# A gathered mixture of experts: the diagonal of gates and activations built on VectorE instead of ScalarE

## The chip, the cores and the metric

The kernel runs on one core of a Trainium2 chip. The metric is the device time of one execution in microseconds. All data are fp32 except indices.

## The reference

The kernel computes two transformer blocks on 256 latent and 256 context tokens of width 1024. The change touches only their last kind of layer, a product-key mixture of experts ("peer"), which runs twice:

```python
def block_fn(xb):                       # 128 tokens of width 1024
    qry = (xb @ w_query).reshape(P, 8, 2, 128)
    s = jnp.einsum('phcd,hckd->phck', qry, sub_keys)
    top_s, top_i = lax.top_k(s, 16)
    cand_s = top_s[..., 0, :, None] + top_s[..., 1, None, :]      # 16 x 16 pairs
    cand_i = top_i[..., 0, :, None] * 128 + top_i[..., 1, None, :]
    best_s, pos = lax.top_k(cand_s, 16)
    idx = jnp.take_along_axis(cand_i, pos, axis=-1)
    gate = jax.nn.softmax(best_s, axis=-1)
    act = jax.nn.gelu(jnp.einsum('pd,phkd->phk', xb, u_tab[idx]))
    coef = gate * act
    return jnp.einsum('phk,phkd->pd', coef, v_tab[idx])
```

Each token picks 8 x 16 = 128 experts. For each it needs a dot product with a row of `u_tab` and adds a multiple of a row of `v_tab`.

## The kernel before

A tile is 128 tokens, one per partition. Layer 0 has four tiles (0 to 3), layer 1 two (here 4 and 5). A row (`ee`, 0 to 127) is one expert for each token of the tile; `q = 128 * n + ee` counts rows in a layer. Each engine runs its own hand-written program; they meet only at semaphores. `wait_ge` waits, `then_inc(*S.up(key))` announces, and `v()` and `a()` add a wait for the engine's own last operation.

For each row:
- GpSimd (POOL, L2893) issues an indirect DMA that fetches 128 rows of 2048 numbers, u and v side by side, 1 MB, into one of seven buffers. It waits for the dot and for the matmuls of the row seven before.
- VectorE (DVE, L2909) multiplies the u half with the tokens and sums it into one column of `acts`: the dot.
- ScalarE (ACT, `act_row`, recorded at L211 as all its operations) makes three operations: GELU of that column into `coef`, `coef` times the column of `gates`, and the identity times `coef`: a 128x128 diagonal in one of four buffers `dg`.
- TensorE (PE, L2863) multiplies the diagonal with the v half in two matmuls of 512 columns (four records), accumulating over all 128 rows in two PSUM banks.

At the end of a tile VectorE waits for the last matmul and adds the result to the tokens (L2920, L2922), and only then starts the next tile's dots.

Beside the rows of a tile the next tile's experts are selected. From row 8 on (row 14 in tile 1) TensorE computes the scores (L2731, L2741) and ScalarE copies them and the next tokens out of PSUM before it turns to the row's own work (`act_select`). VectorE does one piece of `dve_select` per row, behind the dot: 48 rows of MAX8, FIND_INDEX8 and MATCH_REPLACE8 over 128 elements, two rows that add pairs (L2800), 24 rows over 256 elements (L2805 to L2811), 24 rows that look up indices (L2822, L2825, L221), and a few small ones; at row 107 ScalarE takes an Exp for the gates (`act_gates`). Tiles 3 and 5 are the last of their layers and select nothing.

Some rows carry work of neighbouring stages (`beside`): tile 0 and the first rows of tile 1 the latent half of the projection before the layer, its norm and its queries (`pe_late`, `dve_late`, `act_late`, with 16 MB of weights), tile 3 the keys of the attention that follows, tile 5 a part of the final norm.

## Time and profile before

| | |
|---|---|
| time, three runs | 4545.08 us median, 4542.48 to 4550.28 |
| the profiled execution | 4545.08 us, span 4543.3, mean granted TensorE clock 0.939 |
| busy | PE 84%, PEld 47%, DVE 62%, ACT 28%, POOL 26% of the span |
| tiles of experts | 2286 to 2674, 3007, 3331, 3664 us (layer 0); 3877 to 4212, 4534 (layer 1) |
| gathers | 768, 820 MB on the queue they share with GpSimd's other loads |

How to read it: the profile is one execution. An engine is busy while an instruction runs; PE is the matmuls, PEld the weight loads, DVE VectorE, ACT ScalarE, POOL GpSimd. The share of the 16 DMA engines' time is the DMA share. The granted clock is in parts of full speed. In the rows below "idle before" is the time for which the engine stood before the operation, and the arrow names what ended it. All operands lie in one allocation named `arena` (SBUF) or in `bank` (PSUM).

### The profile page before, as it was taken

What the parts mean: (1) busy time and instruction counts of PE and PEld (TensorE: products, weight loads), DVE (VectorE), ACT (ScalarE), POOL (GpSimd) and SP (SyncE); (2) the same over time, 40 slices, a digit from 0 to 9 for tenths busy, and PEclk for the clock granted to TensorE, in tenths of its full rate; (3) what the DMA queues carried; (4) which work ended last, traced back from release to release, by engine and by line L of the source; (5) the groups of instructions that cost most, each with busy time, mean ns of one, the idle gap of its engine ahead of it and who ended that gap; (6) DMA issues with size and microseconds to landing.
All of it is one profiled execution on the core that took longest, in us unless ns stands there. A gap on an engine that the chain in (4) does not pass through costs nothing.

```text
span 4543.3 us, 43290 instructions
## 1 busy us (share of the span) xinstructions
PE 3794.2 (84%) x13554; PEld 2121.6 (47%) x13554; DVE 2832.7 (62%) x5670; ACT 1268.6 (28%) x3341; POOL 1197.0 (26%) x1220
## 2 busy tenths in 40 slices
PE   7879879998878898887879888777779778777777
PEld 3334437643467777676844552232223247322222
DVE  3756447767666677664667747767755546676544
ACT  1231110025311222212133333343333321333333
POOL 0001100001033343331034333333344400333333
PEclk9889999999988999889989999999999989999999
DMA  5423235544200000003289999999999942899998
GB/s 211 176 99 125 100 130 188 219 157 169 88 6 24 5 24 6 26 6 152 83 338 420 384 363 421 421 403 421 422 407 413 422 168 75 345 421 421 407 422 364
DMA packets 140150, 1073.82 MB, mean 236 GB/s; under 512 B 15504, under 2 KB 15888, under 8 KB 21520
## 3 DMA queue, kind: packets, MB, share of 16 engines
q0 software_dynamic: 112608, 820.04, 43.9%
q1 hardware_dynamic: 27312, 251.02, 14.5%
q8 instruction: 107, 1.75, 0.2%
q14 instruction: 123, 1.01, 0.1%
HBM read 1060.51 MB, written 10.49 MB: 236 GB/s over the span
## 4 chain that ended last, share of the span: by engine, by line
PE 39%; DMA 20%; DVE 19%; issue 12%; POOL 7%; ACT 2%; DVEq 0%; POOLq 0%; SPq 0%; ACTq 0%
PE bank L199 19%; DMA arena<-in_uv,arena 18%; POOL arena L2893 6%; PE bank L2863 3%; PE bank L2423 3%; DVE arena L2909 2%; PE bank L2146 2%; DVE arena L443 2%; ACT arena L211 2%; PE bank L2138 2%; PE bank L1620 2%; DVE arena L561 2%; DVE arena L217 2%; DVE arena L221 2%; PE bank L2125 1%
## 5 line engine op out<-in xcount | busy, mean ns | idle before, releaser
L2863 PE MATMUL bank<-arena 128*128 128x512 f32 x3072 | 1492.0, 618 | 390.6 <-ACT arena L211 390.1
L211 ACT ACTIVATE arena<-arena 128x1 f32<-128x1 f32 (+5 forms) x2625 | 866.2, 330 | 2055.2 <-DVE arena L2909 1155.2
L2909 DVE CUSTOM_DVE_ANT_0 arena<-arena 128x1024 f32<-128x1024 f32 x768 | 941.3, 1226 | 703.4 <-DMA arena<-in_uv,arena 690.2
L199 PE MATMUL bank<-arena 128*128 128x128 f32 (+5 forms) x4896 | 1303.7, 426 | 75.2 <-ACT arena L211 35.1
L2863 PEld LDWEIGHTS bank<-arena 128*128 128x128 f32 x3072 | 541.6, 191 | 1314.4 <-ACT arena L211 880.7
L2893 POOL DMA_INDIRECT arena<-in_uv,arena x768 | 772.5, 1006 | 1338.7 <-PE bank L2863 870.1
L199 PEld LDWEIGHTS bank<-arena 128*128 128x128 f32 (+3 forms) x4896 | 816.2, 196 | 551.7 <-issue 424.8
L211 ACT ACTIVATE arena<-bank 128x512 f32<-128x512 f32 (+3 forms) x464 | 248.2, 535 | 1081.3 <-PE bank L2125 503.3
L2208 POOL TENSOR_TENSOR arena<-arena 128x512 f32<-128x512 f32 x128 | 163.5, 1277 | 456.1 <-PE bank L2138 449.2
L443 DVE CUSTOM_DVE_ANT_0 arena<-arena 128x1024 f32<-128x1024 f32 x192 | 240.6, 1253 | 33.8 <-DMA arena<-in_w_rows 22.0
L2146 PE MATMUL bank<-arena 128*128 128x128 f32 x1024 | 159.5, 306 | 88.6 <-DVE arena L2167 88.6
L2146 PEld LDWEIGHTS bank<-arena 128*128 128x128 f32 x1024 | 142.5, 214 | 106.9 <-DVE arena L2167 98.5
L626 POOL TENSOR_SCALAR arena<-arena 128x1 f32<-128x1 f32 (+3 forms) x48 | 15.5, 323 | 648.2 <-ACT arena L211 454.0
L561 DVE SCALAR_TENSOR_TENSOR arena<-bank,arena 128x508 f32<-128x508 f32 (+2 forms) x248 | 159.0, 641 | 8.8
L2167 DVE TENSOR_TENSOR arena<-arena,bank 128x512 f32<-128x512 f32 x128 | 88.0, 687 | 113.2 <-PE bank L2138 106.3
L2138 PE MATMUL bank<-arena 128*128 128x128 f32 x1024 | 141.4, 285 | 2.2 <-issue 2.0
L217 DVE TENSOR_SCALAR arena<-bank,arena 128x256 f32<-128x256 f32 (+3 forms) x162 | 84.0, 518 | 93.3 <-PE bank L520 50.4
L2138 PEld LDWEIGHTS bank<-arena 128*128 128x128 f32 x1024 | 129.1, 196 | 17.2 <-issue 13.0
L211 ACT ACT_TABLE_LOAD x86 | 110.3, 1283 | 80.0 <-DMA arena<-gates_rest 25.3
L2423 PE MATMUL bank<-arena 128*128 128x512 f32 x256 | 131.4, 639 | 0.0
L217 DVE TENSOR_SCALAR arena<-bank 128x512 f32<-128x512 f32 x128 | 88.5, 691 | 42.8 <-PE bank L2146 32.3
L216 DVE TENSOR_SCALAR arena<-bank,arena 128x256 f32<-128x256 f32 (+5 forms) x98 | 55.3, 565 | 77.6 <-PE bank L199 60.8
(250 smaller groups left out, 2800.3 us busy)
## 6 DMA issues: line engine op xcount, KB each, us to landing
arena<-in_w_rows SPq DMA_DIRECT2D x50, 1024.0 KB, 4.9
arena<-in_w_in SPq DMA_DIRECT2D x16, 2048.0 KB, 8.2
arena<-in_wq SPq DMA_DIRECT2D x14, 2048.0 KB, 8.6
arena<-in_dn_w SPq DMA_DIRECT2D x12, 2048.0 KB, 9.0
arena<-in_w_up SPq DMA_DIRECT2D x11, 2048.0 KB, 8.0
arena<-in_dn_wo SPq DMA_DIRECT2D x8, 2048.0 KB, 11.0
arena<-in_w_rows POOLq DMA_DIRECT2D x14, 1024.0 KB, 6.3
arena<-in_uv,arena POOLq DMA_INDIRECT x768, 12.8
```

The costliest lines, as they stand in the source:

```text
L199: t = p.e.matmul(out, l, r, start=(i == 0), stop=(i == n - 1))
L211: return a().activation(out, in_, f, **kw)
L217: return v().tensor_scalar(out, a, s1, s2, op0, op1)
L443: v().tensor_tensor_reduce(trash, w[:, j, :], self.crow[r], 1.0, 0.0, ALU.mult, ALU.add, self.M[m][:, j0 + j, c:c + 1]).then_inc(*(V.up("m ...
L561: t = v().scalar_tensor_tensor(dst[:, :, o], src[:, :, f], wc(d + h), dst[:, :, o], ALU.mult, ALU.add)
L2138: t = p.e.matmul(b[:, H4[h]], N[:, H4[h]], X[:, H4[h]], start=True, stop=True)
L2146: t = p.e.matmul(b[:, H4[h]], m["Y"][d][:, H4[h]], m["XT"][d][k % 2][:, H4[h]], start=True, stop=True)
L2208: g().tensor_tensor(heads(m["N"][d], 4), heads(m["AT"][d][k % 2], 4), bc(m["masks"][:, d, l - 3, :], 1, 4), ALU.mult).then_inc(*G.up("in.N ...
L2423: t = p.e.matmul(b, self.hT[:, q, 128 * i:128 * i + 128], m["zch"][:, q, :], start=(q == 0), stop=(q == 7))
L2863: t = p.e.matmul(by[half], m["dg"][ee % 4], m["uv"][r][:, 1024 + 512 * half:1536 + 512 * half], start=(ee == 0), stop=(ee == 127))
L2893: g.e.indirect_dma_start(out=m["uv"][q % 7], out_offset=None, in_=self.I["uv"], in_offset=bass.IndirectOffsetOnAxis(ap=m["idx"][n % 2][:, ...
L2909: v().tensor_tensor_reduce(self.spare, uv[:, 0:1024], m["ht"][n % 2], 1.0, 0.0, ALU.mult, ALU.add, m["acts"][:, ee:ee + 1]).then_inc(*V.up ...
```

## The change

ScalarE keeps the GELU alone. VectorE builds the diagonal, behind the dot and the selection piece of the same row: one tensor_scalar that multiplies the identity by the column of `coef` and by the column of `gates`. It waits for ScalarE's GELU and for the matmuls of the row four before. TensorE waits for VectorE's `dg` instead of ScalarE's. ScalarE no longer waits for the gates or for a `dg` buffer; from the third tile of a layer it waits for the last diagonal of the tile two before, which read the same `coef` buffer.

```diff
--- before.py
+++ after.py
@@ -2858,7 +2858,7 @@
                 if n + 1 < nt and ee == self.select_row(m["layer"], n):
                     self.pe_select(p, m, k, n + 1, None)
                 r = (128 * n + ee) % 7
-                p.wait_ge(*A.of(k + ".dg", n, ee))
+                p.wait_ge(*V.of(k + ".dg", n, ee))
                 for half in range(2):
                     t = p.e.matmul(by[half], m["dg"][ee % 4], m["uv"][r][:, 1024 + 512 * half:1536 + 512 * half],
                                    start=(ee == 0), stop=(ee == 127))
@@ -2910,6 +2910,11 @@
                                          m["acts"][:, ee:ee + 1]).then_inc(*V.up(k + ".dot", n, ee))
                 if ee >= self.select_row(m["layer"], n):
                     next(ahead, None)
+                v.wait_ge(*A.of(k + ".act", n, ee))
+                if q > 3:
+                    v.wait_ge(*P.of(k + ".y", *divmod(q - 4, 128)))
+                v().tensor_scalar(m["dg"][ee % 4], self.ident, m["coef"][n % 2][:, ee:ee + 1],
+                                  m["gates"][n % 2][:, ee:ee + 1], ALU.mult, ALU.mult).then_inc(*V.up(k + ".dg", n, ee))
                 self.beside(n, ee, side)
             run(ahead)
             i = t0 + n
@@ -2929,25 +2934,16 @@
         self.act_gates(a, m, k, 0)
         self.act_experts(a, m, k, side)
 
-    def act_row(self, a, m, k, n, ee):
-
-        P, V, A = self.P, self.V, self.A
-        q, coef = 128 * n + ee, m["coef"][n % 2][:, ee:ee + 1]
-        a.wait_ge(*V.of(k + ".dot", n, ee))
-        act(a, coef, m["acts"][:, ee:ee + 1], ACT.Gelu).then_inc(*A.up(k + ".act", n, ee))
-        a.wait_ge(*V.of(k + ".gate", n))
-        act(a, coef, coef, ACT.Copy, scale=m["gates"][n % 2][:, ee:ee + 1]).then_inc(*A.up(k + ".coef"))
-        if q > 3:
-            a.wait_ge(*P.of(k + ".y", *divmod(q - 4, 128)))
-        act(a, m["dg"][ee % 4], self.ident, ACT.Copy, scale=coef).then_inc(*A.up(k + ".dg", n, ee))
-
     def act_experts(self, a, m, k, side):
         P, V, A, nt = self.P, self.V, self.A, m["nt"]
         for n in range(nt):
             for ee in range(128):
                 if n + 1 < nt and ee == self.select_row(m["layer"], n):
                     self.act_select(a, m, k, n + 1)
-                self.act_row(a, m, k, n, ee)
+                a.wait_ge(*V.of(k + ".dot", n, ee))
+                if n > 1:
+                    a.wait_ge(*V.of(k + ".dg", n - 2, 127))
+                act(a, m["coef"][n % 2][:, ee:ee + 1], m["acts"][:, ee:ee + 1], ACT.Gelu).then_inc(*A.up(k + ".act", n, ee))
                 if n + 1 < nt and ee == self.select_row(m["layer"], n) + self.SELECT:
                     self.act_gates(a, m, k, n + 1)
                 self.beside(n, ee, side)
```

## Rows read from the trace of the kernel before

**Rows 1.** The page: busy us of each engine, share of the span, instructions.
```profile
PE 3794.2 (84%) x13554; PEld 2121.6 (47%) x13554; DVE 2832.7 (62%) x5670; ACT 1268.6 (28%) x3341; POOL 1197.0 (26%) x1220
```

**Rows 2.** Windows, tiles 0, 5: PE, PEld, DVE, ACT, POOL; clock, DMA share, GB/s.
```profile
2286.00:2674.00 388.00, 344.98 (x1063) 198.37 (x1064) 240.82 (x520) 132.41 (x415) 154.52 (x138) 0.96 0.97 396
4212.00:4534.00 322.00, 253.60 (x512) 88.07 (x512) 162.40 (x263) 116.17 (x386) 116.52 (x124) 0.99 0.98 407
```

**Rows 3.** Timeline of a steady row, tile 2: start, duration, engine, idle before.
```profile
3201.39 1.23 DVE L2909 CUSTOM_DVE_ANT_0 arena<-arena 128x1024 f32<-128x1024 f32 x1 [0.74 <-DMA arena<-in_uv,arena]
3202.66 1.02 ACT L211 ACTIVATE arena<-arena 128x1 f32<-128x1 f32 x3 [1.48 <-DVE arena L2909]
...
3203.74 1.98 PE L2863 MATMUL bank<-arena 128*128 128x512 f32 x4 [0.52 <-ACT arena L211]
3203.88 1.22 DVE L2909 CUSTOM_DVE_ANT_0 arena<-arena 128x1024 f32<-128x1024 f32 x1 [0.26 <-DMA arena<-in_uv,arena]
```

**Rows 4.** The gather's line L2893, issue to landing, all 768.
```profile
DMA to landing us min/median/max: 5.5/12.8/14.2
```

**Rows 5.** Groups of VectorE's dots in tile 0, windows 2478:2513 and 2455:2517.
```profile
L2909 DVE CUSTOM_DVE_ANT_0 arena<-arena 128x1024 f32<-128x1024 f32 x13 | 15.9, 1225 | 2.0 <-DMA arena<-in_uv,arena 0.3
...
L2909 DVE CUSTOM_DVE_ANT_0 arena<-arena 128x1024 f32<-128x1024 f32 x21 | 25.7, 1226 | 8.4 <-DMA arena<-in_uv,arena 6.2
```

**Rows 6.** Groups by form, VectorE, windows 350:370 and 2286:4535 (mean ns).
```profile
L216 DVE TENSOR_SCALAR arena<-arena 128x128 f32<-128x128 f32 x4 | 1.1, 287 | 0.9 <-POOL arena L1193 0.9
...
L2822 DVE TENSOR_TENSOR arena<-arena 128x512 f32<-128x512 f32 x40 | 27.7, 692 | 1.5
L217 DVE TENSOR_SCALAR arena<-bank,arena 128x128 f32<-128x128 f32 x32 | 13.1, 409 | 13.3 <-PE bank L520 10.6
```

**Rows 7.** Timelines of single operations, in four places.
```profile
1246.54 1.27 POOL L2027 TENSOR_TENSOR arena<-arena 128x512 f32<-128x512 f32 x1 [144.37 <-ACT arena L211]
1247.24 0.85 DVE L216 TENSOR_SCALAR arena<-arena 128x512 f32<-128x512 f32 x1
...
1490.51 0.69 DVE L217 TENSOR_SCALAR arena<-bank 128x512 f32<-128x512 f32 x1 [1.92 <-PE bank L2146]
1491.33 0.69 DVE L1995 TENSOR_TENSOR arena<-arena,bank 128x512 f32<-128x512 f32 x1
...
2599.96 0.94 POOL L2893 DMA_INDIRECT arena<-in_uv,arena  x1 [0.32 <-PE bank L2863]
2600.44 0.23 DVE L216 TENSOR_SCALAR arena<-arena 128x128 f32<-128x128 f32 x1
...
3103.74 0.20 ACT L211 ACTIVATE arena<-arena 128x1 f32<-128x1 f32 x1 [1.46 <-DVE arena L2909]
```

**Rows 8.** Timeline of the boundary of tiles 4 and 5.
```profile
4214.78 1.23 DVE L2909 CUSTOM_DVE_ANT_0 arena<-arena 128x1024 f32<-128x1024 f32 x1 [0.17 <-DVE arena L2922]
...
4216.16 1.23 DVE L2909 CUSTOM_DVE_ANT_0 arena<-arena 128x1024 f32<-128x1024 f32 x1
...
4221.18 1.15 POOL L2893 DMA_INDIRECT arena<-in_uv,arena  x1 [8.27 <-PE bank L2863]
```

**Rows 9.** Groups of the dots in tile 4: windows 3928:4029, 4029:4099, 4099:4159, 4163:4209.
```profile
L2909 DVE CUSTOM_DVE_ANT_0 arena<-arena 128x1024 f32<-128x1024 f32 x40 | 49.1, 1226 | 27.2 <-DMA arena<-in_uv,arena 27.2
L2909 DVE CUSTOM_DVE_ANT_0 arena<-arena 128x1024 f32<-128x1024 f32 x27 | 33.1, 1225 | 13.2 <-DMA arena<-in_uv,arena 13.0
L2909 DVE CUSTOM_DVE_ANT_0 arena<-arena 128x1024 f32<-128x1024 f32 x24 | 29.4, 1225 | 12.6 <-DMA arena<-in_uv,arena 12.3
L2909 DVE CUSTOM_DVE_ANT_0 arena<-arena 128x1024 f32<-128x1024 f32 x18 | 22.1, 1225 | 22.5 <-DMA arena<-in_uv,arena 22.5
```

**Rows 10.** Timeline of tile 4 behind row 8.
```profile
3908.84 1.23 DVE L2909 CUSTOM_DVE_ANT_0 arena<-arena 128x1024 f32<-128x1024 f32 x1
...
3912.12 5.25 ACT L211 ACTIVATE arena<-arena 128x1 f32<-128x1 f32 x15
```

**Rows 11.** Timeline of tile 4, row 107.
```profile
4159.11 1.28 ACT L211 ACT_TABLE_LOAD   x1
```

## The prediction

> **What bounds the kernel now.** I read the page first, then the gather stage in windows, a steady stretch as a timeline, the waits of the three lines of an expert row, and the places where the steady state breaks. An expert row is one of the 128 gathers of a tile. In the page [rows 1] TensorE looks like the bound with 84% and VectorE has 62%; ScalarE, which the change relieves, 28%. By tile [rows 2] the reader sees what bounds: the DMA share is 0.97 in tile 0 and 0.98 in tile 5, and 0.99 to 1.00 in the four between, at about 400 GB/s. The gathers' bandwidth sets the pace. In the timeline [rows 3] one row takes 2.48 us (3201.39 to 3203.88). Its chain after the landing is dot 1.23, three ACT operations 1.02 and four matmuls 1.98, 4.3 us with the gaps. A gather takes a median of 12.8 us to land and 5.5 at the least [rows 4]. Seven buffers at 2.48 give a cycle of 17.4 us, so 0.3 lie between the last matmul and the next issue. A row that is late shortens its successor's time in the queue, which can fall from 12.8 to 5.5: a row may be some 6 to 7 us late before the DMA runs dry, and I take 6; less lateness than that costs nothing. VectorE waits for landings [rows 9] and doesn't set the pace, except in tile 0, between 2478 and 2513: there 13 dots had 2.0 us of idle time ahead of them [rows 5], and 0.14 is the gap that remains when nothing is waited for (4214.78 + 1.23 + 0.14 = 4216.16 [rows 8]). VectorE sets the pace there.
>
> **What the change removes.** On ScalarE two of three operations per row, the multiplication by the gate and the diagonal. The three take 1.02 with their gaps, the GELU that stays 0.20: 0.82 less [rows 3, 7]. ScalarE was a third busy, so by itself this is worth nothing. It shortens the path from dot to matmul where VectorE goes straight to the diagonal.
>
> **What it adds to VectorE.** One tensor_scalar of 128x128 with two pointer scalars per row, behind three waits (ScalarE's GELU, TensorE's row four back, its own last operation). No row shows it. Price of the instruction at this shape: SBUF to SBUF with one pointer 0.287, with none 0.23 (2600.44), from PSUM with two 0.409 [rows 6, 7]. I take the middle between the two forms that it lies between, 0.35, and keep 0.23 and 0.41 as the ends. The Trainium skill (VectorE: DVE Perf Modes, "The TRN2 errata") gives 58 cycles plus half a cycle per element here, an estimate of 0.13 us; the 0.23 of the row without pointers already contradicts it, and by it the sum would be about 4543, with everything hidden but tile 0. Price of the waits: a VectorE operation whose line waits for three things, all of them there, starts 0.13 after the last one (1490.51 + 0.69 = 1491.20, next 1491.33) [rows 7]. So a row gains 0.13 + 0.35 = 0.48 us, if the GELU is back in time. It is, in rows with selection work: the GELU ends 0.24 after the dot and most selection pieces take 0.7. Without selection VectorE waits for it: 1.23 + 0.03 + 0.20 + 0.13 + 0.35 + 0.14 = 2.08 against 1.38 now, 0.69 more, still under 2.48.
>
> **Rows with selection.** The dot now shares its 2.48 us with a selection piece and the diagonal. A piece of 0.69 [rows 6] gives 1.23 + 0.03 + 0.69 + 0.13 + 0.35 + 0.14 = 2.57 us, just more than a gather's 2.48; shorter pieces stay below, longer ones go further above. So VectorE is at the bandwidth's pace, and it is the sum over the list that decides. Tile 4, by the idle time ahead of the dots [rows 9], less 0.14 each: 40 rows have 27.2 - 5.8 = 21.4 and need 19.2; 27 rows have 9.3 and need 13.0; 24 rows have 9.1 and need 11.5; then 18 rows without selection have 19.9 and need 12.4.
> Where it starts: at row 8 ScalarE first copies scores and rows, so its GELU begins at 3912.12; VectorE, which went on to dot 9 at 3908.84 [rows 10], now begins that dot at 3912.12 + 0.20 + 0.35 + 0.14 = 3912.8. Everything in its queue stands with it, the next dots and the next selection pieces; TensorE waits for it, and through TensorE the gathers. Row 9 landed one pitch after row 8, at about 3907.1, so its dot is 5.7 us late. Seven rows on, the trace's own DMA has lost 1.1 us at this place, and VectorE at 2.47 a row no more: row 16 is about 4.3 late. Then 4.3 - 2.2 + 3.7 + 2.4 = 8.2 late at row 107. At row 108 the softmax's Exp holds ScalarE for two table loads of 1.28 each [rows 11], which now stops VectorE for 1.5: 9.7. The tail wins back 7.5. The peak exceeds the 6 us allowance by 3.6, and that is DMA time lost. Tiles 1 and 2 run the same list: 3 x 3.6 = **+10.8 us**.
>
> **Tile 0.** It carries the late projection and its norm as well. From 2455 to 2517 the 21 dots have 8.4 - 2.9 = 5.5 us of slack and need 10.1; of the slack 3.7 is one wait at 2468 of which only 1.4 can be used. So 10.1 - 5.5 + 2.3 = **+6.9 us** [rows 5]. Behind it TensorE, busy 345 of the tile's 388 us [rows 2], sets the pace and carries the delay on.
>
> **What it gives back.** Where no selection piece lies between, the matmul starts 2.34 us after the dot's start now (3201.39 to 3203.74) and 1.98 then: 0.36 less. At a row with ScalarE's copies ahead, the two removed operations and their gaps (0.82) are replaced by 0.48, or about 0.5 with the wait. That counts only where a queue is short or a stage ends: at the tile boundaries the gathers stop (POOL idles 8.3 us before 4221.18 [rows 8]) and the dot of row 0 waits for the last y. I count 0.36 at nine such places (row 0 of six tiles, the last y of tiles 1, 3 and 5) and 0.5 at the row with the copies in four tiles: **-5.2 us**. The waits of the added operation on TensorE (row four back) cost nothing where TensorE is ahead of VectorE; where it is behind, VectorE stands, but TensorE has three matrices waiting. The removed four-buffer wait on ScalarE was the same one.
>
> **Sum.** The profiled execution took 4545.08, which is the median too (span 4543.3). 4545.1 + 10.8 + 6.9 - 5.2 = 4557.6, **4558**.
>
> **Rivals.**
> *Hidden by the queue* (chance 0.28). If the second pointer is free (0.29), a row gains 0.42; the 118 rows of a selecting tile need 7 us less, the peak falls below the allowance, and the 10.8 is gone; tile 0 pays 5.6: 4545. With 0.35 but an allowance of 7 instead of 6, the 10.8 is 7.8 and the time 4555. For it: nothing in the rows shows DMA time lost for lateness under 5 us. Against it: one pointer costs 0.06 over none, so a second can hardly be free.
> *Paid back* (0.06), the other side: the shorter chain from dot to matmul lets gathers be issued earlier wherever the queue is thin. The DMA's idle time is 388 x 0.03 + 322 x 0.02 = 18 us in tiles 0 and 5 [rows 2] and a few more in the others; half of it would give 4535. It decides only if a VectorE row gains less than 0.25 us, so that tile 0 is not held; the waits alone take 0.13, and 0.23 is the cheapest instruction seen.
> *The dear diagonal* (0.14): 0.41 us, as from PSUM. 118 rows x 0.06 = 7 us more late in each of three tiles, all beyond the allowance, and 1.6 in tile 0: 4558 + 21 + 2 = 4581.
> *VectorE and GpSimd hold each other* (0.04). A tensor_scalar of 512 elements from SBUF took 0.85 us behind a GpSimd operation that had begun (1246.54, 1247.24), more than the 0.69 of the slower form from PSUM (1490.51) [rows 7]. The diagonals fall 2.1 us behind a dot, where the next gather issue (0.94 us) has begun. Held for its rest, 0.47 on average, 300 selecting rows would cost 141 us: 4700. Against it: the 0.23 operation at 2600.44 ran at its usual speed inside the issue of 2599.96 [rows 7]. The Trainium skill (SBUF — State Buffer, "Who interferes with whom") says that such an operation and GpSimd exclude each other and that descriptors of a GpSimd DMA starve; the row inside the issue speaks against it here, the one beside a GpSimd operation for it.
>
> **Chances and range.** Forecast 0.48, hidden 0.28, dear 0.14, paid back 0.06, held 0.04. A measurement here can tell about 0.2% (9 us) from no change: 4536 to 4554. Hidden lies inside it, and so does the lower fifth of my own case (4550 to 4567 by itself): same 0.38, faster 0.05, slower 0.57. The range takes in the hidden case and the dear one: 4541 to 4583.
>
> **What would show it.** The added line at 0.35 us, 0.13 behind the selection piece; VectorE's dots in 3928 to 4209 with 0.14 ahead of most instead of DMA waits; ScalarE one operation per row of 0.20 instead of three; the DMA share of the selecting tiles down by 0.01; tile 0 longer by 6, the tiles without selection (3 and 5) equal or shorter. I am wrong if the line takes 0.29 or less, if it stretches when a gather issue runs, or if DMA waits remain ahead of the dots throughout the 256-wide pieces.

## The result, and the profile after

The changed kernel takes 4572.01 us (median of 4, 4570.91 to 4575.46), the kernel before 4543.84 beside it: a ratio of 1.0052, 95% interval 1.0028 to 1.0077. It is slower by about 24 to 28 us.

One thing must be cleared away before the traces can be compared. The profiled execution of the changed kernel has a span of only 4540.2 us, shorter than the 4543.3 of before. The difference arises before the first gather, in a stage that the change doesn't touch. Windows of that stage, before first, then the changed kernel, then a second execution of the changed kernel (columns as in [rows 2]):

```profile
1350.00:1960.00 610.00, 531.62 (x3242) 436.50 (x3240) 412.45 (x764) 126.77 (x279) 222.84 (x192) 0.89 0.05 16
```
```profile
1350.00:1960.00 610.00, 534.94 (x3389) 441.07 (x3390) 427.08 (x783) 131.59 (x287) 235.01 (x203) 0.93 0.05 16
```
```profile
1350.00:1960.00 610.00, 527.80 (x3161) 431.48 (x3162) 407.76 (x747) 122.61 (x272) 217.25 (x188) 0.88 0.05 16
```

In the same 610 us TensorE did 3242, 3389 and 3161 matmuls at a granted clock of 0.89, 0.93 and 0.88 of full speed. The first gather was issued at 2286.2, 2255.7 and 2297.2. So all traces here are **aligned**: every time is counted from the first gather's issue, and "behind" means the end of a row's last matmul, less the same in the kernel before. Aligned, the changed kernel ends 27.4 us behind, and its second execution 30.9, in line with the timed difference.

The changed kernel, beside [rows 1] and [rows 4]. First the page's engines:

```profile
PE 3783.4 (83%) x13554; PEld 2105.3 (46%) x13554; DVE 3120.7 (69%) x6438; ACT 734.0 (16%) x1805; POOL 1267.1 (28%) x1220
```

The groups of the dots and of the added line over the whole gather stage (busy us, mean ns, idle us ahead and its releasers):

```profile
L2909 DVE CUSTOM_DVE_ANT_0 arena<-arena 128x1024 f32<-128x1024 f32 x768 | 941.8, 1226 | 278.2 <-DMA arena<-in_uv,arena 202.6 <-DVE arena L2916 1.3
L2916 DVE TENSOR_SCALAR arena<-arena 128x128 f32<-128x128 f32 x768 | 289.0, 376 | 173.1 <-ACT arena L211 113.1 <-PE bank L2863 5.4
```

The added line's own view (ns, min/median/max), and the line of the gathers' view on landing:

```profile
L2916 DVE TENSOR_SCALAR arena<-arena x768: 345/346/582, 2263.0 to 4528.4; 128x128 f32<-128x128 f32 x192
```
```profile
DMA to landing us min/median/max: 5.4/10.7/17.5
```

VectorE is busy for 288 us more, ScalarE for 535 less. The added line costs 346 ns in the median and 582 at most; 173 us of idle time lie ahead of its 768 operations. A gather now takes 10.7 us from issue to landing in the median instead of the 12.8 of [rows 4]. These two views know the landing of only 365 and 184 of the 768 gathers. Over all of them, read from the semaphores as told below, the medians are 10.4 and 12.8 us, and 10.3 in the second execution: the queue is shorter.

Now the windows that answer to [rows 9] (3920:4022, 4022:4093, 4093:4156 and 4158:4206 here), VectorE's dots and the added line in tile 4:

```profile
L2909 DVE CUSTOM_DVE_ANT_0 arena<-arena 128x1024 f32<-128x1024 f32 x42 | 51.5, 1225 | 6.0
L2916 DVE TENSOR_SCALAR arena<-arena 128x128 f32<-128x128 f32 x42 | 14.5, 346 | 5.8
...
L2909 DVE CUSTOM_DVE_ANT_0 arena<-arena 128x1024 f32<-128x1024 f32 x27 | 33.1, 1225 | 3.9
...
L2909 DVE CUSTOM_DVE_ANT_0 arena<-arena 128x1024 f32<-128x1024 f32 x25 | 30.6, 1225 | 3.6 <-DVE arena L2916 0.2
...
L2909 DVE CUSTOM_DVE_ANT_0 arena<-arena 128x1024 f32<-128x1024 f32 x21 | 25.7, 1226 | 3.3 <-DMA arena<-in_uv,arena 0.6
L2916 DVE TENSOR_SCALAR arena<-arena 128x128 f32<-128x128 f32 x22 | 11.4, 517 | 5.8 <-ACT arena L211 5.4
```

The 27.2 us that 40 dots waited for the DMA are 6.0 for 42: 0.14 each, the gap that remains when nothing is waited for. VectorE sets the pace from row 9 of the tile to its last few rows. Ahead of the added operation lie 5.8 / 42 = 0.14.

Where the time goes, by tile (my sums, aligned, us behind the kernel before at the last row):

| | tile 0 | 1 | 2 | 3 | attention | 4 | 5 | end |
|---|---|---|---|---|---|---|---|---|
| predicted, before the give-back | 6.9 | 3.6 | 3.6 | 0 | 0 | 3.6 | 0 | 12.5 with -5.2 |
| changed kernel | 9.8 | +5.5 | +7.0 | +3.3 | -1.7 | +3.0 | +0.5 | 27.4 |
| the same, second execution | 10.1 | +5.4 | +7.4 | +3.5 | +0.5 | +4.0 | 0.0 | 30.9 |

For the experiments I also read when each gather really landed. Each gather raises the semaphore of its buffer 16 times, and the last of these is the landing (in up to 4% of the rows one or more of the 16 are missing from the trace). A dot that waits for nothing but its gather starts 0.02 us behind it. In tile 4, the wait from landing to dot, and in brackets the time from issue to landing (us):

```
row                     8         12        28        60        84        104       116
before               0.0 (13)  0.1 (13)  0.0 (13)  0.0 (14)  0.7 (13)  0.0 (13)  0.0 (12)
changed              0.0 (13)  4.7 (14)  3.7 (9)   2.1 (12)  7.1 (8)   6.9 (6)   2.5 (8)
changed, again       0.0 (13)  4.1 (14)  4.0 (9)   3.1 (11)  7.3 (8)   5.9 (7)   1.5 (9)
load only            0.0 (13)  0.6 (14)  0.1 (13)  0.1 (15)  4.5 (10)  4.0 (9)   0.0 (8)
diagonal first       0.0 (13)  6.3 (14)  7.2 (7)   8.9 (7)  10.4 (6)   9.4 (5)   4.1 (8)
no stand             0.0 (12)  0.0 (14)  0.2 (13)  0.2 (15)  5.1 (10)  6.3 (7)   0.0 (9)
six, changed         0.0 (10)  4.3 (12)  1.9 (8)   0.4 (11)  4.2 (8)   4.1 (7)   0.0 (10)
```

A buffer's cycle is seven rows (six in the last line), so each microsecond of waiting for VectorE is one that the next gather isn't in the queue.

### The profile page after: what moved, and what is told of

The parts are those of the page before. It is cut to its first block, busy times and chain, and to the rows that moved or that the text cites. A ratio compares the mean times of both kernels' runs of the same rounds, so it can differ in the third digit from the quotient of the medians.

```text
span 4540.2 us, 42538 instructions
## 1 busy us (share of the span) xinstructions
PE 3783.4 (83%) x13554; PEld 2105.3 (46%) x13554; DVE 3120.7 (69%) x6438; ACT 734.0 (16%) x1805; POOL 1267.1 (28%) x1220
## 4 chain that ended last, share of the span: by engine, by line
PE 42%; DVE 35%; DMA 9%; issue 7%; POOL 4%; ACT 3%; DVEq 1%; POOLq 0%; SPq 0%; ACTq 0%
PE bank L199 20%; DVE arena L2909 11%; DMA arena<-in_uv,arena 6%; PE bank L2863 5%; DVE arena L2916 4%; POOL arena L2893 3%; PE bank L2423 2%; PE bank L2146 2%; DVE arena L443 2%; ACT arena L211 2%; DVE arena L221 2%; PE bank L2138 2%; DVE arena L217 2%; DVE arena L561 2%; PE bank L1620 2%
## 5 line engine op out<-in xcount | busy, mean ns | idle before, releaser
L2893 POOL DMA_INDIRECT arena<-in_uv,arena x768 | 839.9, 1094 | 1297.2 <-PE bank L2863 631.9
L211 ACT ACTIVATE arena<-arena 128x1 f32<-128x1 f32 (+6 forms) x1089 | 331.7, 305 | 2609.3 <-DVE arena L2909 1819.0
L2916 DVE TENSOR_SCALAR arena<-arena 128x128 f32<-128x128 f32 x768 | 289.0, 376 | 173.1 <-ACT arena L211 113.1
## 6 DMA issues: line engine op xcount, KB each, us to landing
arena<-in_uv,arena POOLq DMA_INDIRECT x768, 10.7
```

What stands on the lines that cost most here:

```text
L211: return a().activation(out, in_, f, **kw)
L2893: g.e.indirect_dma_start(out=m["uv"][q % 7], out_offset=None, in_=self.I["uv"], in_offset=bass.IndirectOffsetOnAxis(ap=m["idx"][n % 2][:, ...
L2916: v().tensor_scalar(m["dg"][ee % 4], self.ident, m["coef"][n % 2][:, ee:ee + 1], m["gates"][n % 2][:, ee:ee + 1], ALU.mult, ALU.mult).then ...
```

## The experiments

Ratios are to the kernel before, with 95% intervals; "aligned" is the end behind it, from one profiled execution each; the kernel before has one trace too. The table shows all of them at the last row of each tile.

```
                          tile 0    1     2     3     4     5 (end)   ratio
changed, again              10.1  15.5  22.9  26.4  30.9  30.9       1.0066 [1.0043, 1.0088]
one pointer                 10.1  17.8  27.2  31.0  36.4  37.3       1.0076 [1.0044, 1.0109]
load only                    6.7   8.7  13.1  13.4  16.4  17.3       1.0041 [1.0022, 1.0060]
a row behind                16.9  25.8  38.2  43.7  49.0  52.2       1.0138 [1.0111, 1.0166]
not in selecting rows        0.3  -0.9  -1.1   2.5  -1.1   0.8       1.0007 [0.9991, 1.0023]
not in tile 0                3.4   9.3  17.2  22.0  23.8  24.9       1.0048 [1.0030, 1.0066]
later on ScalarE             3.4   4.6   6.0   7.2   8.7  11.2       1.0020 [1.0005, 1.0034]
diagonal first              13.8  35.3  58.1  60.9  81.2  82.2       1.0171 [1.0146, 1.0197]
six in flight, before        0.5   2.7   9.0  17.8  19.5  22.3       1.0062 [1.0039, 1.0084]
six in flight, changed      13.0  22.1  32.4  47.3  53.9  57.3       1.0120 [1.0088, 1.0152]
no stand                    10.1  14.2  18.9  23.4  23.4  25.7       1.0033 [1.0005, 1.0061]
hybrid                      -0.3  -2.4  -0.9   0.9  -1.8   0.7       0.9985 [0.9969, 1.0001]
```

**The scatter.** The changed kernel once more, unedited.

> The changed kernel once more, for the scatter of the aligned differences: if they are good to a few us it shows +24 to +31 aligned, with tile 0 at +9 to +11, and a median of 4568 to 4576; then the +37 of the one-port form and the +17 of the load alone are differences. If it comes out at +17 or at +37, they are not.

Up to row 383 the two executions agree within 0.6 us at each tile's end, at the very end within 3.5. Where VectorE sets the pace, differences within a tile are good to about 1 us; elsewhere they are not: in "not in tile 0" below, tile 0 has the code of the kernel before and is 3.4 us longer. The end is good to 3 or 4. So by the traces the load alone (+17) differs from the change, and so does the one-pointer form (+37), by a little; the intervals of the timed ratios overlap in both cases.

**Load only.** The kernel before, and on VectorE an operation of the added form that nothing waits for.

```
+                v().tensor_scalar(self.spare[:, 0:128], self.ident, m["acts"][:, ee:ee + 1],
+                                  m["gates"][n % 2][:, ee:ee + 1], ALU.mult, ALU.mult).then_inc(...)
```

> The kernel before, ScalarE still makes the diagonal; VectorE makes a tensor_scalar of the same form and size behind each selection piece into unused space, which nobody waits for and which waits for nobody but VectorE's own last operation. Its value is not used. Theory LOAD: VectorE's time per row grows by 0.35 + 0.03 instead of 0.48, and that alone costs counted from the first gather 10 to 20 us (tile 0 about 7, tiles 1, 2 and 4 together 5 to 12). Theory WAIT (the cost is that VectorE stands until ScalarE's GELU is back, at row 8 behind the copies, at row 108 behind the Exp, and in every row without selection): at most 5 us here.

+17.3 aligned, within the expected 10 to 20. VectorE's time alone is worth about 60% of the loss. The operation is nearly as dear as in the change (358 ns in the mean for 376) but stands 0.03 behind its predecessor; ahead of the change's lie 0.14 and more.

**A row behind.** The changed kernel, with each diagonal behind the next row's dot, when the GELU has long been done.

```
+                if ee:
+                    self.dve_diag(v, m, k, n, ee - 1)
                 if ee >= self.select_row(m["layer"], n):
                     next(ahead, None)
-                v.wait_ge(*A.of(k + ".act", n, ee)) ... tensor_scalar(...)
```

> The changed kernel with VectorE building the diagonal of the row before, right behind the dot and ahead of the selection piece, so that the GELU has had a row's time. The load stays (0.35 + 0.13 per row), the standing for the GELU goes (113 us in all, 365 times), the matmul of a row starts about 1 to 1.5 us later than in the changed kernel. Theory WAIT: counted from the first gather at most 15 us over before instead of 27. Theory LOAD: 22 to 30, for the waits for the GELU fall mostly in rows that had slack. Later matmuls cost 1 to 2 us at each of six tile ends in either.

The waits for the GELU are all but gone (13.5 us in place of 113), and it costs 25 us more than the change: +52.2, where the two theories said at most 15 and 22 to 30. The time is saved where it isn't short: in tile 2 the added work takes 64 us of VectorE instead of 74, but in the rows with selection 52 instead of 53. Against that each diagonal, and so each buffer, comes a dot later: the issue that a dot releases ends 6.33 us behind the dot's end, 4.47 in the change.

**Later on ScalarE.** The converse: VectorE as before, and ScalarE makes each diagonal later by two more copies of the coefficient.

```
+        for again in range(2):
+            act(a, coef, coef, ACT.Copy).then_inc(*A.up(k + ".again"))
```

> The kernel before with two more copies of the one-element coefficient in ScalarE's row, so that the diagonal is ready about 0.4 us later in every row and VectorE has nothing more to do. If the load on VectorE alone makes the loss, and lateness is under cover of the queue, this is the kernel before: aligned at the first gather 0 to +2. If the lateness of the diagonals, and so of the release of the rows' buffers, makes the 10 us by which the change exceeds the load alone (+27 against +17), it is about +8 to +12.

+11.2 aligned, and the ratio says 1.0020. But this is not the missing piece between +17 and +27, as I had it. From the end of a dot to the end of the gather issue that it releases, the median is 4.31 us before, 5.78 here, and only 4.47 in the changed kernel. The dose of lateness is ten times that of the change. Per selecting tile from tile 1 on it costs 1.2 to 1.6. The dose is so large for a reason that the timeline of GpSimd's issues and VectorE's dots in this kernel shows:

```profile
3301.70 1.23 DVE L2909 CUSTOM_DVE_ANT_0 arena<-arena 128x1024 f32<-128x1024 f32 x1 [1.25 <-DMA arena<-in_uv,arena]
3301.79 1.94 POOL L2893 DMA_INDIRECT arena<-in_uv,arena  x1 [0.54 <-PE bank L2863]
```

And the view of the gathers' line:

```profile
L2893 POOL DMA_INDIRECT arena<-in_uv,arena x768: 932/1925/2129, 2280.5 to 4521.2; - x192
```

The issue begins 0.09 after the dot and takes 1.94 instead of 0.94; 1.925 is now the median.

**Diagonal first.** The changed kernel, with the diagonal ahead of the row's selection piece: VectorE stands for the GELU in every row.

> The changed kernel with each diagonal ahead of the row's selection piece: VectorE stands for GELU in every row, 0.37 us in place of the 0.13 us gap, and the diagonal is ready about 0.45 us earlier in the rows with a selection piece. If VectorE's time per row is what counts, those rows cost 0.24 us more and the end is later than the change's by 5 to 25 (+32 to +50 aligned). If lateness of the diagonal is what counts, the end is equal or earlier, +15 to +27.

+82.2, three times the change, and far above the 32 to 50 that I expected. Groups of tile 2, from its first to its last dot, in the kernel before, the change, the load alone and this kernel:

```profile
L2909 DVE CUSTOM_DVE_ANT_0 arena<-arena 128x1024 f32<-128x1024 f32 x128 | 156.8, 1225 | 84.6 <-DMA arena<-in_uv,arena 82.2 <-DVE arena L2922 0.2
```
```profile
L2909 DVE CUSTOM_DVE_ANT_0 arena<-arena 128x1024 f32<-128x1024 f32 x128 | 156.9, 1226 | 18.7 <-DVE arena L2916 0.5
L2916 DVE TENSOR_SCALAR arena<-arena 128x128 f32<-128x128 f32 x127 | 48.6, 383 | 25.0 <-ACT arena L211 10.9 <-PE bank L2863 0.5
```
```profile
L2909 DVE CUSTOM_DVE_ANT_0 arena<-arena 128x1024 f32<-128x1024 f32 x128 | 156.9, 1226 | 36.4 <-DMA arena<-in_uv,arena 22.3 <-DVE arena L2913 0.5 <-DVE arena L2924 0.2
L2913 DVE TENSOR_SCALAR arena<-arena 128x128 f32<-128x128 f32 x127 | 46.7, 367 | 4.6
```
```profile
L2909 DVE CUSTOM_DVE_ANT_0 arena<-arena 128x1024 f32<-128x1024 f32 x128 | 157.0, 1226 | 19.2 <-DVE arena L2825 0.5 <-DVE arena L2782 0.5 <-DMA arena<-in_uv,arena 0.2
L2914 DVE TENSOR_SCALAR arena<-arena 128x128 f32<-128x128 f32 x127 | 49.7, 391 | 41.3 <-ACT arena L211 36.7 <-PE bank L2863 4.6
```

Before, the dots of tile 2 waited 84.6 us, of which 128 x 0.14 = 18 can't be used: VectorE had 67 us to give. The load alone takes 46.7 + 4.6 = 51 of them, and the tile is 4.4 us longer. The change takes 48.6 + 25.0 = 74, 7 too many, and the tile is 7.0 longer. Diagonal first takes 49.7 + 41.3 = 91, which is 24 too many; the tile is 22.8 longer. That looks like a rule, but it is in part bookkeeping: once no dot waits for a landing, a tile's length is the sum of VectorE's pieces. And it fails elsewhere. Tiles 1 and 4 had 76 and 78 us to give, the change takes 73 in each, and they are still 5.5 and 3.0 longer; "a row behind" takes 64 of the 67 in tile 2, and the tile is 12.4 longer. Room in rows without selection is of no use to the rows with it.

So the tile has to be split. The 102 rows from the first with selection to the last, my sums in us: what the dots' idle time left to give before (less 0.14 each), what the added operation takes with the idle time ahead of it, how far behind the last of these rows ends, counted from the tile's start, and how far behind the tile ends.

```
                        takes, tiles 1, 2, 4    behind, last such row    behind, tile's end
to give, before           43.6  42.8  44.2
load only                 41.8  41.7  41.7          7.0   8.7   7.8        2.0   4.4   3.0
changed                   53.2  53.5  53.2          9.0  11.1   7.8        5.5   7.0   3.0
one pointer               56.0  56.3  55.7         11.7  13.0  10.6        7.8   9.4   6.2
diagonal first            73.6  71.3  71.1         24.2  26.2  24.3       21.4  22.8  20.3
```

This is the reading that settles the sizes. In the change VectorE is 9 to 11 us short in these rows, in every tile alike, and it comes out of them 8 to 11 us behind; diagonal first is 27 to 30 short and comes out 24 to 26 behind. The rows without selection that follow win 3 to 5 us back. The load alone is within its sum and yet falls behind, because the long pieces stand together: 7 to 8 us of idle time are left unused in its earlier rows.

**One pointer.** The changed kernel with a form that reads one pointer scalar and a broadcast row.

```
-  v().tensor_scalar(m["dg"][ee % 4], self.ident, coef, gates, ALU.mult, ALU.mult)
+  v().scalar_tensor_tensor(m["dg"][ee % 4], self.ident, coef, gates.to_broadcast([128, 128]), ALU.mult, ALU.mult)
```

> The changed kernel with its diagonal built by scalar_tensor_tensor (identity times coef times gates, the gate column broadcast) in place of tensor_scalar: two inputs, one element per cycle, not the form that was seen to take 0.58 us instead of 0.35 inside a gather issue. Counted from the first gather issue, the changed kernel needs 27.4 us more than the one before. Theory HOLD (GpSimd's gather issue holds the tensor_scalar 102 times by 0.235 us, and the reverse): the new form takes 0.35 to 0.42 us at all times, none near 0.58; gather issues of 1.9 us get rarer; counted from the first gather 15 to 22 us over before if it takes 0.35, about 27 if 0.41. Theory LOAD (only the 0.48 us of VectorE per row counts, the holds fall where there is slack): 27 us or more, following the mean duration alone.

This form is at about 350 ns in 607 rows and at 380 to 420 in the others, and never at 580: mean 362 in place of 376. It isn't faster; it ends at +37.3. The table above shows why. Its dear executions fall into the rows with selection, where the mean is 0.375 to 0.379 in tiles 1, 2 and 4 against 0.346 in the change; that makes 2.5 to 2.8 us more per tile there, and the tiles end 2.3 to 3.3 later than the change's. The 99 stretched diagonals of the change fall almost all (96) into rows without a selection piece. So they are not what the change loses by.

**Six in flight.** Each gather waits for the row six back instead of seven, which takes 2.49 us from the cycle; in the kernel before and in the changed one.

```
-                    u, e = divmod(q - 7, 128)
+                    u, e = divmod(q - 6, 128)
```

> The kernel before with one buffer's worth less of lead: each gather waits for the row six back, not seven, so a cycle is 14.9 us in place of 17.4 and a gather's time from issue to landing falls by 2.5 us in the steady stretches, from about 12.3 to 9.8. If the DMA keeps its pace as long as that time is above 7.5 to 8, the steady stretches keep their 2.487 us per row, and only the places where it is thin now (tile ends, TensorE's side pieces, tile 0) lose up to 2.5 each: +15 to +50 us in all. If a row is already late for free only down to 10 or so, every row is slower and the sum is above +60.

> The changed kernel with the same cut. If lateness is free up to an allowance and costs its excess (my reading: about 5 us with seven buffers, so about 2.5 with six), tiles 1, 2 and 4 each lose up to 2.5 more than they do with seven: the change costs +33 to +37 over the kernel with six, where it costs +27 to +31 with seven. If VectorE's own pace is the whole price, the difference stays at +27 to +31; if it falls below +20, the six-buffer kernel had already lost the same time elsewhere.

The kernel before loses 22.3 and keeps its 2.49 us per row in the steady stretches, with 10.3 us from issue to landing. The change then costs 57.3 - 22.3 = 35.0, the number that an allowance gave, but not at the expected place. Tiles 1, 2 and 4, which should have lost up to 2.5 more each, lose 6.8, 4.0 and 4.0 through the change, together 15 as with seven buffers (15.5). The 7.6 us more lie in tile 0 (12.5 for 9.8), in tile 3 (6.1 for 3.3) and in the attention stage (0.9 for -1.7). So the hit is luck, and this pair doesn't confirm the allowance. What it shows is in the table of tile 4: at rows 84 and 104 the wait for VectorE is 4.2 and 4.1 instead of 7.1 and 6.9, while the time in the queue is 8 and 7 us against 8 and 6. The queue gives way down to about the same floor.

**No stand.** The changed kernel, but ScalarE builds the diagonals of the rows that follow its own long pieces, so that VectorE never stands for them.

```
+        row = self.select_row(m["layer"], n)
+        return n + 1 == m["nt"] or ee - row not in (0, 1, 2, 3, self.SELECT + 1, self.SELECT + 2, self.SELECT + 3)
```

> The changed kernel, but in the four selecting tiles ScalarE still builds the diagonals of the four rows behind its copies and of the three rows behind the gates' Exp, so VectorE doesn't stand there. Where it stands, the wait from landing to dot jumps from 0.5 to 5.2 us in tile 4 and 4 us of it stay until row 60. If lateness adds up to the peak, as the prediction has it, the wait starts at about 1 and the peaks fall by 3 to 4: tiles 1, 2 and 4 lose 1 to 3 us less each, +18 to +23 aligned. If the second half of the list alone sets the loss (VectorE over 2.49 us per row there until the wait saturates), it is the change, +26 to +31.

Tiles 1, 2 and 4 lose 4.1, 4.7 and 1.8, together 10.6 where the change loses 15.5: each falls by 1.2 to 2.3, within the expected 1 to 3. The end is at +25.7, not at the expected 18 to 23; tiles 3 and 5 lost 3 us more than in the change, though no row of theirs is built otherwise. In them the two executions of the change agree within 0.6 us, so this isn't explained. Row 12 of tile 4 doesn't wait for VectorE, where the change waits 4.7 (the 0.5 and 5.2 of the expectation count from the last DMA packet, 0.5 us ahead of the semaphore), and rows 84 and 104 wait 5.1 and 6.3 for 7.1 and 6.9. The peak was to fall by 3 to 4 and is as high as in the change (7.1 for 7.2). The 256-wide pieces bring most of the lateness by themselves.

**Not in tile 0.** VectorE's diagonals only from row 13 of tile 1 on.

> Diagonals of tile 0 and of the first 13 rows of tile 1 are left on ScalarE, all later ones are VectorE's as in the change. If tile 0's loss is simply added to the rest (VectorE is behind there and nothing gives it back), the end counted from the first gather's issue is +27.4 less the 9.8 of tile 0, +17 to +18, and the median is near 4562. If what tile 0 loses is only work that a later tile would have lost anyway (one shared stock of lead), the end stays at +25 to +27.

+24.9. Tile 0 loses 3.4 in place of 9.8, though its code is that of the kernel before, and 2.8 of it stood at row 56; from row 56 on it loses 0.6, where the two executions of the change lose 8.1 and 8.2. The later tiles lose 21.5, where the change loses 17.6 and 20.8. My +17 to 18 fell: of the 6.4 us saved in tile 0, 2.5 are left at the end against one execution of the change and 6.0 against the other. How much of a tile's gain lasts is not settled by this.

**Not in selecting rows.** VectorE builds the diagonal only in rows without a selection piece.

```
+    def on_vector(self, m, n, ee):
+        row = self.select_row(m["layer"], n)
+        return n + 1 == m["nt"] or not row <= ee <= row + self.SELECT + 2
```

> VectorE builds the diagonal only in rows without a selection piece (rows 0 to 7 and 110 to 127 of tiles 0, 2 and 4, the corresponding rows of tile 1, all of tiles 3 and 5); in all others ScalarE makes the three operations as before. Theory LOAD (the prediction's own terms): the 24 us of tiles 0, 1, 2 and 4 are gone and the shorter path from dot to matmul pays back 2 to 4 us: counted from the first gather -4 to 0 against before. Rival: the 3.3 us that tile 3 lost without any selection stay, for VectorE still pays 0.69 us per row there and the keys of the attention are prepared on it: +2 to +6.

+0.8: the loss is gone, and with it most of what there was to gain. So VectorE's time in the rows with selection is what the change loses by. Tile 3 still loses 3.6, as in the change, and tile 3 has no selection; tile 5 loses 1.9, more than in the change. The timeline of the changed kernel's VectorE, rows 28 to 31 of tile 3:

```profile
3393.73 0.35 DVE L2916 TENSOR_SCALAR arena<-arena 128x128 f32<-128x128 f32 x1 [0.27 <-ACT arena L211]
3394.18 2.09 DVE L217 TENSOR_SCALAR arena<-bank,arena 128x256 f32<-128x256 f32 x4
3396.42 1.23 DVE L2909 CUSTOM_DVE_ANT_0 arena<-arena 128x1024 f32<-128x1024 f32 x1
...
3398.41 1.23 DVE L2909 CUSTOM_DVE_ANT_0 arena<-arena 128x1024 f32<-128x1024 f32 x1
...
3400.41 1.23 DVE L2909 CUSTOM_DVE_ANT_0 arena<-arena 128x1024 f32<-128x1024 f32 x1
...
3401.91 0.58 DVE L2916 TENSOR_SCALAR arena<-arena 128x128 f32<-128x128 f32 x1 [0.27 <-ACT arena L211]
```

A plain row takes 1.99 now (3396.42 to 3398.41). Every third row evicts a bank for the next stage, about 2 us more, so three rows take 8.4 (the dots of rows 29, 32 and 35 start at 3396.42, 3404.83 and 3413.25) where the gathers bring three in 7.46. By row 38 the dots are 3 us late. By itself that is inside any allowance. But three rows on, TensorE has a side piece:

```profile
3431.85 7.03 PE L199 MATMUL bank<-arena 128*128 128x512 f32 x16
3438.72 8.75 PE L2863 MATMUL bank<-arena 128*128 128x512 f32 x20
```

Before the change that pause alone takes the gathers from 12.7 us in the queue to 5.4, so nothing is left for 3 us more: rows 49 to 51 land with 3.55, 3.57 and 3.28 between them (2.46, 1.94 and 2.88 before), and that is 3.1 of the 3.3 us. In the second execution they are 4.17, 3.38 and 3.61.

**Hybrid.** The kernel just told, and in tile 3 rows 24 to 45 left on ScalarE.

```
+        return not row <= ee <= row + self.SELECT + 2 if n + 1 < m["nt"] else not (m["layer"] == 0 and 24 <= ee <= 45)
```

> VectorE's diagonals only in rows without a selection piece, as in the earlier such kernel (+0.8 aligned, of which tile 3 had lost 3.6), and in tile 3 ScalarE keeps rows 24 to 45, where three VectorE operations of 1.9 us fall every third row. If those rows make VectorE late and TensorE's side piece of 5.8 us behind row 41 has used up the queue's allowance, tile 3 loses nothing and the end is at -3 to -1.5 aligned, with the rows up to 383 as in the earlier one. If tile 3's loss comes from elsewhere, it is +0.8 again.

Rows 49 to 51 of tile 3 land with 2.47, 2.47 and 2.59 between them: the loss at that place is gone, so the diagonals of rows 24 to 45 cause it. That TensorE's pause is the other half is read from the trace and was not tested. The tile as a whole still ends 1.8 later, in small steps elsewhere (0.9 at row 30, 0.5 at row 115, 1.8 at the end), so only half of the 3.6 is won, and the end of +0.7 isn't the -1.5 I expected. The ratio is 0.9985 [0.9969, 1.0001]: no gain that can be told from none. There is no version among these that beats the kernel before.

## Why the prediction was right, and where not

Direction and mechanism held, and the places but one (tile 3). The size did not hold well: +12.5 us forecast, +27.4 measured in the traces. The 4572 lies inside the range only because the range took in the dear rival (4581). The shortfall of 14 us comes from several terms of the sum.

*The row's price, 0.48: right.* The instruction takes 0.346 (0.35 predicted) and follows 0.14 behind a selection piece (0.13); in the plain rows with selection of tiles 1, 2 and 4 the two make 0.483 to 0.487. The estimate of 0.13 from the Trainium skill (VectorE: DVE Perf Modes, "The TRN2 errata") is off by more than a factor of two against 0.346; that section says itself that its row under-predicts. The mean over tile 2 is higher, 0.58, but that is no fault of the price: it mixes in the stand at row 8 (4.0 with the instruction) and the 26 rows without selection, which take 0.75 to 0.81 and have room for it. The room was rightly read too: 21.4 + 9.3 + 9.1 = 39.8 us for 91 rows, 0.44 a row, where the trace of before gives 0.42 to 0.43 over all 102. In rows without selection I was 0.09 too high: 2.08 predicted, 1.99 measured, because the 0.13 of the waits runs beside the GELU.

*The stand at row 8: right.* The timeline of tile 4, beside [rows 10]:

```profile
3905.01 0.20 ACT L211 ACTIVATE arena<-arena 128x1 f32<-128x1 f32 x1
3905.25 0.35 DVE L2916 TENSOR_SCALAR arena<-arena 128x128 f32<-128x128 f32 x1 [3.66 <-ACT arena L211]
...
3905.74 1.22 DVE L2909 CUSTOM_DVE_ANT_0 arena<-arena 128x1024 f32<-128x1024 f32 x1
```

VectorE stands for 3.66 us. Predicted were 5.7 late at row 9 and 4.3 at row 16; the waits are 5.3 and 3.7, in the second execution 5.4 and 4.1.

*The peak in tile 4: the number right, the way partly luck.* The 9.7 at row 108 show as 8.6 at row 107: 7.2 of waiting and 0.7 of landing time already lost (5.3 and 2.7 in the second execution). Tile 4 lost 3.0 and 4.0 in the two, 3.6 predicted (9.7 less 6 is 3.7). But most of it is not lost at the peak: at row 84 the dots wait 7.1 and 7.3, more than the allowance, and the landings have lost nothing yet; about 2.5 us go in rows 109 to 118, while VectorE is catching up.

*"Tiles 1 and 2 run the same list: 3 x 3.6": the step that failed most.* They lost 5.5 and 7.0. The list is the same, and VectorE is about as short in each tile (table above); the state in which it starts isn't. In tile 4 the gathers of rows 6 to 8 take 12 to 14 us to land before the change and after. In tile 2 the gathers of rows 7 and 8 take 6 and 8 before the change, 7 and 6 after it, and there the dot of row 8 waits 1.9 for VectorE and that of row 9 6.9 (5.3 in tile 4). At row 107 tile 2 is 11.9 behind in both executions, tile 4 8.6 and 8.7.

*The allowance of 6 us: no such constant.* It came from the shortest gather of all, which is a gather issued after a pause. In tiles 1 to 5 of the changed kernel, the 182 gathers that took 10 to 13 us landed 2.53 apart in the mean, the 123 of 8.5 to 10 us 2.55, the 121 of 7 to 8.5 us 2.67 and the 46 of 5 to 7 us 2.81. In rows 77 to 119 of tile 1, where VectorE sets the pace, the gathers take 8.3 in the mean and no less than 6.9, and land 2.57 apart, 2.51 before. So time is lost bit by bit as the queue gets shorter, and at some places not even a wait of 7 us costs any. In tile 3 TensorE's own pause had used the queue up. What decides between these was not found.

*Tile 0: +6.9 predicted, 9.8 and 10.1 measured.* "Not in tile 0" gives back 6.4 of them, near the 6.9, but that is luck: its tile 0 lost 2.8 by row 56, the change's only 1.8 and 1.9. From row 56 on, where VectorE sets the pace, the change loses 8.1 and 8.2 and that kernel 0.6, so the term was 7.5 to 8, and what was lost ahead of row 56 is not in the sum. It may be scatter, for "hybrid" is only 0.2 behind there.

*The give-back of 5.2: a term for which no run shows anything.* Tile 5, without selection, is 0.5 and 0.0 longer, tile 3 3.3 longer. The attention stage between is shorter by 1.7 in one execution and longer by 0.5 in the other. In the two kernels that build the diagonal on VectorE only where it is short, tile 1 is 1.2 and 2.1 shorter, and the end is at zero. The shorter path from dot to matmul is real only in tiles 3 and 5 (the matmul starts 1.91 after the dot, 2.34 before), and behind it nearly always stands a landing. In the selecting tiles the matmul starts later than before, 2.49 for 2.35, because the diagonal stands behind the selection piece.

*The sum.* 27.4 less 12.5 is 14.9: tile 0 2.9, tiles 1 and 2 5.3, tile 4 -0.6, tile 3 3.3, and 4.0 of the give-back that didn't come.

*The rivals.* "Hidden by the queue" failed on the price: with a second pointer at 0.346 VectorE has no room in the rows with selection. "Dear" (4581) is nearer to the measured 4572 than my own 4558, but not for its reason: the instruction takes 0.346, not 0.41. "They hold each other" is half true, and cheap. The timeline of the catch-up at the end of tile 4:

```profile
4179.36 1.23 DVE L2909 CUSTOM_DVE_ANT_0 arena<-arena 128x1024 f32<-128x1024 f32 x1
4180.86 0.58 DVE L2916 TENSOR_SCALAR arena<-arena 128x128 f32<-128x128 f32 x1 [0.27 <-ACT arena L211]
4181.59 1.23 DVE L2909 CUSTOM_DVE_ANT_0 arena<-arena 128x1024 f32<-128x1024 f32 x1
```
```profile
4179.47 1.92 POOL L2893 DMA_INDIRECT arena<-in_uv,arena  x1 [0.30 <-DVE arena L2916]
4181.69 1.93 POOL L2893 DMA_INDIRECT arena<-in_uv,arena  x1 [0.30 <-DVE arena L2916]
```

The issue starts 0.11 into a dot and lasts 1.92; the diagonal starts inside it and takes 0.58, and so on for rows, at 2.23 us a row instead of 1.99. I had named stretching as a sign that I would be wrong. Of the 205 diagonals that started inside an issue 99 were stretched, by 0.235 and not by the rest of the issue, 23 us of VectorE in all, and 96 of them in rows without a selection piece. The one-pointer form, free of it, was no faster. The rule of the Trainium skill (SBUF — State Buffer, "Who interferes with whom"), that such operations and GpSimd exclude each other, is borne out only in part: the other 106 ran at their usual speed inside an issue.

## What to carry to other kernels

Before work is moved to an engine that "only waits for DMA", add up the idle time ahead of its lines, take off the gap that always remains, and compare it with the whole price of the new work, its waits included. Do it for the stretch in which the engine carries its other work, not for the whole tile: here VectorE had 43 us to give in the 102 rows with selection, and 42 cost 2 to 4 us per tile, 53 cost 3 to 7, 71 to 74 cost 20 to 23, while the sum over the tile said of two tiles that there was room. Don't take the queue's allowance as one number from the shortest gather of all, and look for the other engines that spend it. And of identical tiles compute each with its own starting state.

## What was not expected of the hardware

- A gather issue that begins while a dot runs is held until the dot ends. Its time by how much of the dot was left, all issues of the changed kernel: none running 0.956 us (601), 0.2 to 0.4 left 1.11 (15), 0.4 to 0.6 1.33 (17), 0.6 to 0.8 1.52 (16), 0.8 to 1.0 1.74 (15), 1.0 to 1.2 1.91 (80). An issue that begins together with the dot, in its first 0.03 us, isn't held: 0.97 (11). In "later on ScalarE" 426 issues were held for 1 us each.
- Which diagonals a gather issue stretches is no chance. In the two executions of the change and in "diagonal first", all 329 that began 0.40 to 0.54 us before the end of the issue they fell into took longer, nearly always 0.58 instead of 0.346, and none of the 463 that began elsewhere inside an issue did.
- The DMA share doesn't show the loss. The windows of tile 2, before and after: the share stays at 1.00 while the rate falls from 415 to 405 GB/s and the tile grows by 7 us.

```profile
3009.90:3328.00 318.10, 253.55 (x548) 92.48 (x548) 225.31 (x486) 120.62 (x390) 123.33 (x126) 0.99 1.00 415
```
```profile
2994.70:3320.00 325.30, 256.74 (x547) 92.16 (x548) 274.05 (x613) 32.21 (x136) 138.91 (x126) 0.99 1.00 405
```

- In the changed kernel the median pitch of landings is 2.48 to 2.49 us whether a gather takes 7 us or 14; only the mean rises, by single gaps that are 0.5 to 1.8 us longer. What makes these gaps was not found.
- The stages ahead of the gathers took up to 41 us more or less from one execution to the next (the first issue stands at 2255.7 to 2297.2), with a granted clock of 0.88 to 0.93 in one of them. Without the alignment, the profile would have shown the slower kernel as the faster.
